# One hybrid S5 / Fourier / MoE layer on one core: the first two stages as one program, with the input table in four units

## What is computed

```python
sh1, sc1, g1, sh2, sc2, g2 = adaln(cond, w_ada, b_ada)      # silu(cond) @ w_ada + b_ada
h = rms_norm(x, norm1_g) * (1.0 + sc1) + sh1
proj = h @ w_in                                             # [u_s5 768 | u_f 256 | gates 2048]
ar, ai, bbr, bbi = s5_discretize(lam_re, lam_im, log_dt, b_re, b_im)
for d in range(2):                                          # forward, backward
    bu = einsum("gph,blgh->blgp", bb[d], u)                 # 48 groups of 16 channels, 64 states
    h_r, h_i = s5_scan(ar[d], ai[d], bu_r, bu_i, reverse=d == 1)
    y += Re(C[d] h)
gl = sigmoid(proj[..., 1024:])
```

## Time and profile before

| | us |
|---|---|
| runs | 1071.26, 1071.33, 1075.12 |
| median | 1071.33 |
| the profiled execution, its own time | 1073.07 |
| its span in the profile | 1071.3 |
| TensorE matmuls, busy | 921.2 (86%) |
| VectorE busy | 447.4 (42%) |
| ScalarE busy | 187.9 (18%) |
| GpSimd busy | 116.8 (11%) |

### The profile page before, as it was taken

The page is one execution under the profiler, slowest core; times in us unless marked ns, Lnnn a source line. Parts: engine busy times, 40 slices in busy tenths (PEclk is TensorE's granted clock), DMA queues, the critical chain, the costliest instruction groups (busy, mean ns, idle before and its releaser), DMA issues. The chain is left out here.

```text
span 1071.3 us, 14156 instructions
## 1 busy us (share of the span) xinstructions
PE 921.2 (86%) x5564; PEld 494.7 (46%) x5564; DVE 447.4 (42%) x1059; ACT 187.9 (18%) x394; POOL 116.8 (11%) x119
## 2 busy tenths in 40 slices
PE   2649319899999899997979998998998989989993
PEld 2224117576557655543654533543533535435442
DVE  3799980125981213325432332223223223223246
ACT  4210001342003300014132111111121121111112
POOL 4499960000000000000000000000000000000000
PEclk9769759799999899997989999999999999999997
DMA  9926403602105371201089989999999999999951
GB/s 268 408 84 238 157 1 119 197 2 80 40 1 189 152 289 60 117 1 59 1 362 383 427 331 427 426 418 426 409 426 426 414 427 426 425 425 427 422 227 61
DMA packets 50267, 272.50 MB, mean 254 GB/s; under 512 B 5755, under 2 KB 14363, under 8 KB 21811
## 3 DMA queue, kind: packets, MB, share of 16 engines
q1 hardware_dynamic: 48694, 267.31, 61.3%
q10 hardware_dynamic: 896, 3.46, 1.2%
q0 software_dynamic: 608, 0.80, 0.4%
HBM read 268.30 MB, written 3.24 MB: 253 GB/s over the span
## 5 line engine op out<-in xcount | busy, mean ns | idle before, releaser
L1590 PE MATMUL bank<-sb 128*32 128x512 f32 (+2 forms) x1024 | 197.3, 601 | 3.4 <-DMA sb<-w 3.4
L1590 PE MATMUL bank<-sb_W,sb 128*32 128x512 f32 (+1 forms) x448 | 91.4, 633 | 14.1 <-issue 14.1
L1611 PE MATMUL bank<-sb 128*32 128x512 f32 (+2 forms) x512 | 98.3, 596 | 2.6 <-ACT sb L1677 2.6
L1567 PE MATMUL bank<-sb_Y,sb_ST 128*128 128x512 f32 x324 | 85.6, 416 | 6.8 <-DVE sb L1949 4.8
L765 PE MATMUL bank<-early 128*128 128x384 f32 x256 | 89.8, 499 | 0.0
L1590 PEld LDWEIGHTS bank<-sb 128*32 128x32 f32 (+2 forms) x1024 | 56.3, 116 | 66.0 <-issue 65.7
L1627 PE MATMUL bank<-sb_S,sb_H 128*128 128x512 f32 (+1 forms) x336 | 78.9, 394 | 6.2 <-ACT sb_H L1712 4.0
L1755 DVE TENSOR_TENSOR sb<-sb,bank 128x512 f32<-128x512 f32 x78 | 53.6, 687 | 63.4 <-PE bank L1567 62.9
L1567 PEld LDWEIGHTS bank<-sb_Y,sb_ST 128*128 128x128 f32 x324 | 57.6, 193 | 39.8 <-issue 12.8
L1627 PEld LDWEIGHTS bank<-sb_S,sb_H 128*128 128x128 f32 x336 | 63.4, 194 | 24.7 <-issue 5.0
L1857 DVE TENSOR_TENSOR sb_Y<-bank,sb_Y 128x512 fp32r<-128x512 f32 x54 | 37.3, 691 | 72.8 <-ACT sb_Y L1682 72.7
(11 more groups left out here) (292 smaller groups left out, 1169.3 us busy)
## 6 DMA issues: line engine op xcount, KB each, us to landing
sb<-w SPq DMA_DIRECT2D x156, 1024.0 KB, 17.4
sb_W<-w SPq DMA_DIRECT2D x36, 1024.0 KB, 14.9
early<-w_ada SPq DMA_DIRECT2D x24, 1024.0 KB, 18.0
early<-w_in SPq DMA_DIRECT2D x12, 1024.0 KB, 8.6
sb<-w_out SPq DMA_DIRECT2D x1, 4096.0 KB, 17.1
sb<-ada_dram SPq DMA_DIRECT2D x6, 512.0 KB, 15.5
early<-w_proj_s SPq DMA_DIRECT2D x1, 2560.0 KB, 16.0
early<-w_glu SPq DMA_DIRECT2D x1, 2304.0 KB, 8.5
```

Source lines behind the costliest of these rows:

```text
L1567: ins = nc.tensor.matmul(bank[m % 2][:, :], ST[:, p, j * P:(j + 1) * P], YR[:, x, p % 2, 512 * h:512 * h + 512], start=p == ps[0] and x == ...
L1590: ins = nc.tensor.matmul(bank[2 + p % 2][c0:c0 + w, :], XT[:, c, P * p + c0:P * p + c0 + w], slot13[k][:, :, c, :], start=c == 0, stop=c = ...
L1611: ins = nc.tensor.matmul(bank[y_bank[p][h]][c0:c0 + w, :], hidT[:, f, c0:c0 + w], slot2[k][:, f, 512 * h:512 * h + 512], start=f == 0, sto ...
```

## The change

The two programs become one. BP is kept in two buffers, each for one of four units: (d = 0, first 12 pairs), (d = 1, first 12 pairs), and the same for the second 12. A group is now two neighbouring pairs q of one direction, so there are again 24 groups of four transposes and eight products, six per unit. The chunk form of u is made for each tile f as soon as it is there (by_chunk, turned), in the order u, some ada chunks, chunk form. After three tiles come the twelve groups of the first two units (unit_groups), the lag kernels 0 to 2, then u 3 to 5 with ada part 2, z, the other twelve groups, lag kernels 3 to 5, and the gates, all 16 behind the last group. The banks of u, lag kernels and z follow one list (MID), two banks in turn. ScalarE makes all copies out of PSUM in the groups and the chunk form. VectorE builds units 0 and 1, then corrects lag kernels 0 to 2, then builds units 2 and 3 in the same buffers, then starts the scan when v_ok says that all sums are copied.

The ring has eight slots for ada part 0, four for u's and z's w_in, four others in turn for ada 1 and 2, and five for the gates' w_in, which now queue behind ada on the same list. B and C are loaded as 48 rows by ScalarE's queue; C is turned by 64 small products with eight copies of B and C on ScalarE in front of the load of x's third tile. d_skip comes as a row and is turned with the parameters. Unit 0 of BP is built whole before hT, where three of four levels of both halves stood before.

The diff, cut to what is spoken of:

```diff
-        BP = at(o_A, 12288).rearrange("p (r n s h) -> p r n s h", r=2, n=DQ, h=GH)
+        UQ = Q // 2
+        BP = at(o_A, 6144).rearrange("p (u r n s h) -> p u r n s h", u=2, r=2, n=UQ, h=GH)
...
+        U = at(o_U, G * NC).rearrange("p (g k) -> p g k", g=G)
+        Uc = at(o_T, 2048, slice(0, NC)).rearrange("p (b n) -> p b n", b=2)
+        V = at(o_V, 2 * DQ * NC).rearrange("p (d r q k) -> p r d q k", d=2, r=2, q=Q)
+        GLT = at(o_A + 6144, 16 * TOK).rearrange("p (m t) -> p m t", m=16)
...
-        ring = [at(o_W + 2048 * n, 2048) for n in range(NR)] + [at(o_T, 2048)]
+        ring = [at(o_W + 2048 * n, 2048) for n in range(NR)] + [at(o_A + 6144 + 2048 * n, 2048) for n in range(3)]
         ada_items = [("ada", b, c) for b in range(3) for c in range(KC + 1)]
...
+        items = ada_items[0:KC + 1] + [("in", 0, c) for c in range(4)] + ada_items[KC + 1:] + [("gate", 0, n) for n in range(8)]
+        slot_of = [n % 8 for n in range(KC + 1)] + [1, 2, 3, 4] + [(5, 6, 7, 0)[n % 4] for n in range(2 * (KC + 1))] + [
+            (1, 2, 3, 4, 0)[n % 5] for n in range(8)]
...
+        UNITS = [(d, half) for half in range(2) for d in range(2)]
+        GROUPS = [(u, d, half * UQ + 2 * k) for u, (d, half) in enumerate(UNITS) for k in range(UQ // 2)]
+        NG = len(GROUPS)
+        MID = [("u", 0), ("u", 1), ("u", 2), ("kk", 0), ("kk", 1), ("kk", 2), ("u", 3), ("u", 4), ("u", 5),
+               ("z", 0), ("z", 1), ("z", 2), ("kk", 3), ("kk", 4), ("kk", 5)]
...
+                for r, name in enumerate(("c_re", "c_im")):
+                    act.dma_start(C_rows[:, r], i[name][0].rearrange("d (q a) h n -> (d q) (a h n)", a=2)).then_inc(s_c, 16)
+                act.dma_start(g1n, i["norm1_g"][0].rearrange("(p c) -> p c", c=KC)).then_inc(s_dg, 16)
+                act.dma_start(g2n, i["norm2_g"][0].rearrange("(p c) -> p c", c=KC)).then_inc(s_dg, 16)
...
+                def table_rows(n):
+                    act.wait_ge(bt_T, n + 1)
+                    if n >= 4:
+                        act.wait_ge(v_mm, n - 3)
+                    nc.scalar.activation(BT[:, n % 4].rearrange("p q r n -> p (q r n)"), bank[1 + n % 2][:, :], ACT.Copy
+                                         ).then_inc(bt_ok, 1)
+
+                def sum_cols(n):
+                    _, d, q = GROUPS[n]
+                    act.wait_ge(v_mm, n + 1)
+                    ps = bank[5 + n % 2][:, 0:4 * NC].rearrange("p (q r k) -> p r q k", q=2, r=2)
+                    for r in range(2):
+                        ins = nc.scalar.activation(V[:, r, d, q:q + 2, :], ps[:, r] if d == 0 else ps[:, r, :, ::-1], ACT.Copy)
+                    ins.then_inc(v_ok, 1)
+
+                def unit_groups(n0, n1):
+                    table_rows(n0)
+                    for n in range(n0, n1):
+                        if n + 1 < n1:
+                            table_rows(n + 1)
+                        sum_cols(n)
+
...
+                u_rows(0)
+                u_rows(1)
+                chunk_rows(0)
+                u_rows(2)
+                chunk_cols(0)
+                chunk_rows(1)
+                chunk_cols(1)
+                chunk_rows(2)
+                chunk_cols(2)
+                act.wait_ge(ada_out, 64)
                 ada_rows(1)
-                act.wait_ge(ada_out, 128)
-                w = (LC - 1) * GH
-                for j in range(NT):
-                    for f in (2 * j, 2 * j + 1):
-                        act.wait_ge(kk_mm, f + 1)
-                        nc.scalar.activation(KK[:, f, 0:w], bank[kk_bank[f % 3]][:, 0:w], ACT.Copy)
-                        nc.scalar.activation(KK[:, f, w + GH:KW], bank[kk_bank[f % 3]][:, w + GH:KW], ACT.Copy).then_inc(kk_act, 1)
-                    act.wait_ge(z_mm, j + 1)
-                    nc.scalar.activation(Z[:, j, :], bank[5 + j % 2][:, 0:DF], ACT.Copy).then_inc(z_ok, 1)
+                act.wait_ge(cp_step, CP_M0)
+                act.wait_ge(cpad_ok, 2)
+                unit_groups(0, NG // 2)
+                for f in range(3):
+                    kernel_cols(f)
+                u_rows(3)
+                u_rows(4)
+                chunk_rows(3)
+                u_rows(5)
+                chunk_cols(3)
+                chunk_rows(4)
+                chunk_cols(4)
+                chunk_rows(5)
+                chunk_cols(5)
...
+                def table(n):
+
+                    u, d, q = GROUPS[n]
+                    if n % (NG // 4) == 0:
+                        pe.wait_ge(bp_ok, u + 1)
+                    if n % (NG // 2) == 0:
+                        pe.wait_ge(uc_ok, 6 if n == 0 else 2 * FT)
+                    if n >= 2:
+                        pe.wait_ge(bt_ok, n - 1)
...
+                u_chunk(0)
+                ada(1, 0)
+                ada(1, 1)
+                ada(1, 2)
+                u_chunk(1)
+                by_chunk(0)
+                ada(1, 3)
+                ada(1, 4)
+                u_chunk(2)
+                turned(0)
+                by_chunk(1)
+                ada(1, 5)
+                ada(1, 6)
+                turned(1)
+                by_chunk(2)
+                ada(1, 7)
+                ada(1, 8)
+                turned(2)
+                unit_groups(0, NG // 2)
                 pe.wait_ge(cpad_ok, 2)
-                pe.wait_ge(bp_ok, 2)
-                pe.wait_ge(ada_row, 2)
+                for f in range(3):
+                    lag_kernels(f)
...
+                def lag_zero(f):
+                    dve.wait_ge(kk_act, f + 1)
+                    w = (LC - 1) * GH
+                    stt(out=KK[:, f, w:w + GH], in0=const[:, C_M16:C_M16 + GH], scalar=dsk[:, f:f + 1],
+                        in1=mid_bank("kk", f)[:, w:w + GH], op0=ALU.mult, op1=ALU.add).then_inc(kk_ok, 1)
...
+                bp_unit(1)
+                for f in range(3):
+                    lag_zero(f)
+                dve.wait_ge(bt_T, NG // 2)
+                bp_unit(2)
+                bp_unit(3)
+                for f in range(3, FT):
+                    lag_zero(f)
+                dve.wait_ge(v_ok, NG)
+
                 scan_c, scan_l = sem("scan_c"), sem("scan_l")
```

More of the change, by code:

```diff
@@ L244, in load @@
                     kind, b, c = items[n]
[L245 to L249, removed]
+                    before = [items[m] for m in range(n) if slot_of[m] == slot_of[n]]
+                    if before and before[-1][0] == "ada":
+                        sp.wait_ge(ring_used, ada_items.index(before[-1]) + 1)
+                    elif before and before[-1][0] == "in":
+                        sp.wait_ge(z_mm, NT)
+                    elif before:
+                        sp.wait_ge(gl_mm, 2 * before[-1][2] + 2)
                     dst = ring[slot_of[n]]
@@ new lines, in by_chunk @@
+                def by_chunk(f):
+                    pe.wait_ge(u_ok, f + 1)
+                    if f == 3:
+                        pe.wait_ge(bt_ok, NG // 2)
+                    elif f:
+                        pe.wait_ge(uc_ok, 2 * f)
+                    for half in range(2):
+                        for k in range(4):
+                            ins = nc.tensor.transpose(bank[1 + half][0:NC, k * P:(k + 1) * P], uT[:, f, 4 * half + k:TOK:LC], ident)
+                        ins.then_inc(uc_T, 1)
@@ new lines, in _ @@
+                ada(2, 7)
+                ada(2, 8)
+                turned(5)
+                for j in range(NT):
+                    z_rows(j)
+                unit_groups(NG // 2, NG)
+                for f in range(3, FT):
+                    lag_kernels(f)
+                for m in range(16):
+                    gates(m)
+                pe.wait_ge(fin_ok, 1)
+                for r in range(2):
+                    ins = nc.tensor.transpose(bank[2][0:DQ, r * P:(r + 1) * P], fin[:, r], ident)
@@ new lines, in _, with kernels @@
+                ins.then_inc(fin_T, 1)
+                def kernels(f):
+                    for half in range(2):
+                        if f >= 1:
+                            pe.wait_ge(t_ok, 2 * (f - 1) + half + 1)
+                        for k in range(4):
+                            t = 4 * half + k
+                            c0 = GH * (LC - 1 - t)
+                            ins = nc.tensor.transpose(bank[4 + half][:, k * P:(k + 1) * P], KK[:, f, c0:c0 + P], ident)
+                        ins.then_inc(t_T, 1)
@@ L514, in _ @@
+                pe.wait_ge(kk_ok, FT)
+                kernels(0)
+                for f in range(FT):
+                    if f + 1 < FT:
+                        kernels(f + 1)
+                    outputs(f)
             @block.vector
@@ L641, in _ @@
                     ins.then_inc(hT_ok, 1)
-                for half in range(2):
-                    bp_level(0, 4, half)
-                dve.wait_ge(ct_ok, 7)
+                dve.wait_ge(ct_ok, 8)
                 for r in range(2):
```

542 lines of the change are left out of this document (240 added, 302 removed).

## The result

| | before | after |
|---|---|---|
| median of four runs each, on one chip, us | 1071.62 | 1018.85 |
| lowest and highest | 1071.26, 1075.12 | 1016.74, 1019.57 |
| the profiled execution, its own time | 1073.07 | 1019.57 |
| its span | 1071.3 | 1017.8 |
| TensorE, VectorE, ScalarE busy | 921.2, 447.4, 187.9 | 917.1, 409.5, 199.1 |

The ratio is 0.9497 (95% interval 0.9473 to 0.9522): 51 to 56 us faster. Busy time hardly changed on TensorE (4 us), so nearly all of the gain is waiting that is gone.

The account below looks back on a forecast made before the run. The prediction took TensorE to bound the rewritten stages wherever it is not waiting. Gains of -54.0 and added costs of +9.3 made -44.7 us, from the median of 1071.33 to 1026.6 us; range 1018 to 1053.

Parts of the forecast that it names:

- border: TensorE's wait where the two programs meet (191.83 us) goes: -3.3 us.
- wait for BP: TensorE's wait before the first lag kernels goes, as BP's halves are needed at different times: -39.7 us.
- waits for w_ada: TensorE's waits in front of w_ada chunks go, with four slots instead of two for ada 1 and 2: -3.2 us.
- chunk form: The 96 transposes of u, alone at mixed clock before, now lie between u and ada products: -3 us.
- pairs and gates, with ScalarE's row copy and the clock: Sums and gates -4.8, ScalarE's work before the first table copy +1.9, cold starts +3 us.
- hand-overs: Short steps between u, chunk form and copies hand over about 20 times at 0.1 us: +2 us (0 to 4).
- start of u: Later tile landing and unit 0 built before hT delay u to 69.4 us: +2.4 us (0 to 6).
- Added waits: ScalarE's queue before the first table copy +1.9, hand-overs +2, cold starts at u and around the groups +3 us.
- Every later stage starts behind it, in unchanged code: A microsecond off TensorE's path before 322 us is one off the end; nothing further counted for later stages.
- The clock: Rival: the clock falls during the groups of transposes and narrow products: +24.4 us, 1051 us; chance 0.24.
- Late tables: Rival: GpSimd still at CP during units 2 and 3, so TensorE waits 20 us for tables: 1047 us; chance 0.06.
- Serial groups: Rival: ScalarE's table copies cannot run under the sums, groups take 3.5 us: 1087 us, slower than before; chance 0.03.

Follow-up runs that it names:

- the padding: The changed kernel with 52 one-column copies added to VectorE's queue at 29 us: 1020.81 us (ratio 0.9521).
- the version with three edits: Changed kernel with second ada row copy behind first groups, CP's levels 1, 2, 4 held for BP's unit 0, x's third tile loaded earlier: 1005.60 us (0.9381).

## Why the prediction was right, and where it was wrong

The direction, the cause and the largest term were right: the wait of 39.7 us went in full, and the border's 3.3 with it. The forecast of 1026.6 was too slow by 8 to 9 us; the median lies just inside the lower end of the range of 1018 to 1053, and the ratio times 1071.33 (1017.4) just below it. Term by term, from the two profiled executions:

| term | predicted | in the traces |
|---|---|---|
| wait for BP | -39.7 | -39.7 |
| waits for w_ada | -3.2 | -4.0 (all ada chunks: 20.8 to 16.8) |
| border | -3.3 | -3.3 |
| chunk form | -3 | -5.1 (14.8 to 9.7) |
| pairs and gates, with ScalarE's row copy and the clock | -4.8 + 1.9 + 3 = +0.1 | +1.3 (115.2 to 116.5) |
| lag kernels, u and z | 0 | -4.2 |
| hand-overs | +2 | +1.4 within the groups (in the row of pairs and gates), none found elsewhere |
| start of u | +2.4 | +5.2 |
| up to the gates' end | -44.7 | -49.8 |
| behind it | 0 | -3.7 |

**"Added waits", the step that failed.** It charged +3 for new cold starts and credited nothing for the one that goes. The new half clock was there and cost what was allowed (3.5 groups x 0.88 = 3.1 us). But with 39.68 us of standing still gone, the lag kernels run at the full clock (6.19 for three, where two took 6.48): the first two alone gave back 2.2 us. I had written that "the one at 157.16 goes" and gave it no number. The rest of the -4.2 for lag kernels, u and z does not come from that wait: 0.9 of it lies in the first u tile and 1.1 in small pieces. The hand-overs sit inside the group, 1.19 us instead of 1.13, which makes 1.4 over 24 groups where 2 were charged.

**"The chunk form: -3."** It was mis-sized by 2.1: the 96 transposes took 9.7 us in all, where the estimate had 11.5 and its gain was rounded down.

**"Every later stage starts behind it, in unchanged code."** This is the second step that failed: it put what follows the gates at nothing, and 3.7 us came there. The shift arrived in full, but the code's place in VectorE's stream changed, and the wait that this shortened gave 2.25 us of it; with the padding the wait was back. The remaining 1.5 us I can't place.

**The start of u** was +5.2 instead of +2.4, within the bound I had given. The tile's sum began at 42.33, the late end of my estimate for its landing, and unit 0 another 4.9 us later. The rows before had 4.8 us there too (33.89 to 38.71), so a landing at 38 to 42 meant a start at 43 to 47 and not the 42 to 45 that I took. Only the chain behind it was as forecast (19.6 us for unit 0). Unit 1 took 31.4 us, inside 19 to 35. That the first tables started at 103.6 and 168.7, where 104 and 169 were forecast, was luck: u began 2.8 us later than forecast, and the stretch from there to the first table took 31.4 us instead of 35; after that the first twelve groups and three lag kernels took 25.4 instead of 22, and the stretch to the next table 39.7 instead of 43.

**The rivals.** The clock did fall, for 3.5 groups, and came back among transposes and narrow products alone; with the wait in front of them taken away, it did not fall in the groups. The Trainium skill (TensorE: Matmul & The Clock Gate, Part 4: PE-mode transpose) has transposes not counting as activity; by it I estimate about 24 us for the twelve groups of the second half (12 x 2.02), and they took 14.5 at a granted clock of 1.00. The measurement decides. Late tables did not come, but the room was small: forcing unit 1 to be late cost 35.9 us, and in the version with three edits unit 3 was late by 2.5. Serial groups did not come either: a group took 1.19 us with the sums copied by ScalarE or by VectorE.

**What the prediction did not ask** is how much of the gain needs the change. It named GpSimd as the cause and then credited the units. Moving GpSimd's loop alone gave 38 us.

## What to carry to other kernels

When one engine's share of a stage is several times its cost alone, find who works beside it before rearranging the consumer: moving the neighbour's loop to a stretch where the first engine is idle may give most of the gain of a rewrite. When a long wait is removed, price what stood cold behind it as a gain, and look for the short waits that remain, since one of 2 us cost 4.4 here. A part that comes ahead of its use by a few microseconds is hidden only until the edits in front of it succeed.

## What the runs showed of the hardware

- VectorE's short instructions wait for whole GpSimd instructions: 0.25 us became 1.5 beside products of 768 columns (1.47 us), so a scan of many short steps nearly stopped for 29 us (191.44 to 220.6), while long products of the same engine slowed only to about 2.2 (from 0.95).
- The granted clock fell to 0.5 behind TensorE idle times of 2.04 and 31.30 us, and before the change behind one of 0.83 us with smaller gaps ahead of it; it did not fall behind the single ones of 0.33 and 0.25 us in front of the groups. It came back while only transposes and 48-column products ran.
- A stall put down to issue, at VectorE's exit from a loop 1000 us into the program, was at most 1.63 us and became 3.92 when 52 tiny instructions were added near the start. How it depends on their number is not shown.
